# Prompt attention of a hybrid decoder step on one core: group A normalised on its probabilities by GpSimd, group B by spread matmuls as before

## The chip, the cores and the metric

One NeuronCore of a Trainium2 chip runs the whole program. The metric is device time in microseconds of one execution; the time of a kernel is the median of several runs. TensorE (PE) multiplies matrices into PSUM banks, VectorE (DVE) and ScalarE (ACT) read and empty them, GpSimd (POOL) works on SBUF, and SyncE (SP) issues DMAs. Each engine runs its own queue in order, and they wait for one another only through semaphores.

## The reference, cut to what matters

```
m = max(s, axis=-1)                 # group A: also with the head's sink
p = exp(s - m[..., None])
den = sum(p, axis=-1)               # group A: plus exp(sink - m)
o = einsum('nbcgqs,nbscd->nbqcgd', p, vc)
o = o / den                         # one denominator for each query row and head
```

Layer 0 mixes 1,024 prompt tokens with attention of 16 heads of width 64: group A (8 heads, the last 128 keys) and group B (8 heads, three dilated windows, merged into one set of weights). A projection, a pooling layer and two MLPs stand around it, and 64 sample tokens take the same way. All of it is float32.

## The kernel before

The program is a row of stages, each a block of engine queues with a barrier at its end: projection, prompt attention, sample attention, output projection, then a trunk of MLPs and pooling. Only prompt attention (`prompt_attention`) is touched. The next stage issues its loads behind the barrier.

It walks over 8 query tiles of 128 rows, called blocks 0 to 7 here. A block has 16 *steps*, one for each head: steps 0 to 7 are group A (pairs A0 to A3), steps 8 to 15 group B (pairs B0 to B3). A head of group A reads 128 keys in block 0 and 256 in the others; a head of group B reads i + 1 key tiles in block i, up to 1,024 columns.

- PE computes the scores of a pair at each even step (`scores`). Where they are wider than 512 columns (group B of blocks 4 to 7, "wide") they fill all four score banks, and the next `scores` waits until both reductions of the pair before are done (`biased_before`). Narrow scores have two sets of banks and wait for the reductions one pair earlier.
- DVE reduces: one custom instruction adds the bias table, writes the scores to `probs` and the row's extreme to `least` (L886). In group A a copy of one column stands ahead of it (L881). ACT exponentiates the row in place and writes its sum to `den` (L848). `probs` has 7 slots (`SB`); a slot is written again when PE has transposed what it held.
- PE transposes the probabilities, 128 columns at a time (`turn`, L947), about five steps late (`LAG`). ACT or DVE copies the result to `pT` (L832, L899), and PE multiplies it with the values (`multiply`, L966). The work is cut into *groups* of up to two key tiles of a pair. A list gives each group a number n, which decides its PSUM bank (4 + n % 2). PE handles groups in *batches* of two consecutive numbers, 2m and 2m + 1: it transposes both, then multiplies the two groups before them. A batch runs at the step of its second group.
- The denominators belong to query rows, while the outputs lie transposed. So a *spread* group follows the last pair of each 8 heads in that list: 8 matmuls of the reciprocals, broadcast to 64 columns, with the identity (L937). ACT copies the bank to `spread` (L827), and DVE multiplies the outputs of 8 heads by it when it takes them out of PSUM (`take_outputs`, L862).
- POOL computes the low parts of keys and queries (L810): three instructions at step 9 for the next block, one at step 1 for group B.

## Time and profile before

| | |
|---|---|
| median of 3 runs | 2415.77 us (2414.3 to 2416.92) |
| profiled execution, its own time | 2418.88 us |
| its span, first to last instruction | 2416.8 us |
| mean granted TensorE clock | 0.971 of full |
| prompt attention, first scores to last outputs | 271.2 to 467.3 us |

The profile shows one execution. PE's matmuls are pipelined and their ends are modelled, so the distance from one group's start to the next group's start is a better price than a duration. The trace splits the matmuls of a spread group and of `multiply` into two records each: 8 of them are x16 there, while 8 transposes are x8.

### The profile page before, as it was taken

What the parts mean: (1) busy time and instruction counts of PE and PEld (TensorE: products, weight loads), DVE (VectorE), ACT (ScalarE), POOL (GpSimd) and SP (SyncE); (2) the same over time, 40 slices, a digit from 0 to 9 for tenths busy, and PEclk for the clock granted to TensorE, in tenths of its full rate; (3) what the DMA queues carried; (4) which work ended last, traced back from release to release, by engine and by line L of the source; (5) the groups of instructions that cost most, each with busy time, mean ns of one, the idle gap of its engine ahead of it and who ended that gap; (6) DMA issues with size and microseconds to landing.
All of it is one profiled execution on the core that took longest, in us unless ns stands there. A gap on an engine that the chain in (4) does not pass through costs nothing.

```text
span 2416.8 us, 34453 instructions
## 1 busy us (share of the span) xinstructions
PE 2276.5 (94%) x14141; PEld 2047.3 (85%) x14141; DVE 960.3 (40%) x1691; ACT 670.3 (28%) x1305; POOL 156.4 (6%) x200
## 2 busy tenths in 40 slices
PE   6999899878796999999999999989999999999997
PEld 6999777666586998989989988878899898998996
DVE  4200266555453342433433434574334243343345
ACT  4211486433332220311311203253022031131121
POOL 1000121000022000000000000441000000000002
PEclk9999899989898999999999999898999999999999
DMA  4230200298322220210201204122022021020123
GB/s 158 74 92 1 88 2 2 83 331 315 114 87 74 70 62 9 69 46 23 69 21 48 61 9 160 41 97 84 7 70 61 9 69 46 24 69 20 50 86 110
DMA packets 125665, 175.94 MB, mean 73 GB/s; under 512 B 14461, under 2 KB 94389, under 8 KB 125436
## 3 DMA queue, kind: packets, MB, share of 16 engines
q1 hardware_dynamic: 121532, 169.86, 21.5%
q10 hardware_dynamic: 4032, 4.65, 0.6%
q8 instruction: 73, 1.20, 0.2%
q14 instruction: 28, 0.23, 0.0%
HBM read 156.14 MB, written 18.58 MB: 72 GB/s over the span
## 4 chain that ended last, share of the span: by engine, by line
PE 66%; DVE 1%; issue 1%; ACT 0%; POOL 0%; DMA 0%; POOLq 0%; ACTq 0%; DVEq 0%
PE ps L1732 31%; PE ps L1752 31%; PE ps L2238 2%; PE ps L2255 1%; PE ps L1741 1%; DVE t_y L1519 0%; DVE t_zn L1519 0%; PE ps L2266 0%; ACT junk L1507 0%; POOL stats L224 0%; DMA t_raw<-mlp_w 0%; PE ps L1790 0%; DVE m_xT_lo L2149 0%; DVE t_y L1690 0%; DVE t_h_lo L1664 0%
## 5 line engine op out<-in xcount | busy, mean ns | idle before, releaser
L1690 DVE TENSOR_TENSOR t_y<-t_y,ps 128x512 f32<-128x512 f32 x288 | 197.4, 687 | 648.7 <-PE ps L1752 648.5
L1752 PE MATMUL ps<-t_w_hi,t_h_hi 128*128 128x512 f32 x1152 | 451.3, 392 | 3.7 <-DVE t_h_hi L1667 2.2
L1752 PE MATMUL ps<-t_w_lo,t_h_hi 128*128 128x512 f32 x1152 | 449.7, 390 | 0.0
L1752 PE MATMUL ps<-t_w_hi,t_h_lo 128*128 128x512 f32 x1024 | 399.6, 390 | 0.0
L1732 PE MATMUL ps<-m_xT_hi,t_w_hi 128*128 128x384 f32 x1512 | 334.2, 329 | 8.8 <-DVE t_w_lo L1651 8.8
L1732 PE MATMUL ps<-m_xT_lo,t_w_hi 128*128 128x384 f32 x1512 | 333.8, 328 | 0.0
L1732 PE MATMUL ps<-m_xT_hi,t_w_lo 128*128 128x384 f32 x1512 | 333.7, 328 | 0.0
L1621 ACT ACTIVATE t_relu<-ps 128x384 f32<-128x384 f32 (+1 forms) x192 | 87.9, 458 | 820.5 <-PE ps L1752 776.7
L1732 PEld LDWEIGHTS ps<-m_xT_hi,t_w_hi 128*128 128x128 f32 x1512 | 259.6, 188 | 10.3 <-DVE t_w_lo L1651 9.2
L1651 DVE TENSOR_TENSOR t_w_lo<-t_raw,t_w_hi 128x1024 fp32r<-128x1024 f32 x128 | 155.4, 1224 | 284.4 <-ACT t_w_hi L1609 284.0
L1752 PEld LDWEIGHTS ps<-t_w_hi,t_h_hi 128*128 128x128 f32 x1152 | 217.2, 189 | 52.2 <-DVE t_y L1690 3.1
L1732 PEld LDWEIGHTS ps<-m_xT_lo,t_w_hi 128*128 128x128 f32 x1512 | 258.7, 188 | 0.0
L1732 PEld LDWEIGHTS ps<-m_xT_hi,t_w_lo 128*128 128x128 f32 x1512 | 258.7, 188 | 0.0
L1752 PEld LDWEIGHTS ps<-t_w_lo,t_h_hi 128*128 128x128 f32 x1152 | 217.2, 189 | 44.4
L1752 PEld LDWEIGHTS ps<-t_w_hi,t_h_lo 128*128 128x128 f32 x1024 | 193.0, 188 | 40.4
L1609 ACT ACTIVATE t_w_hi<-t_raw 128x1024 fp32r<-128x1024 f32 x128 | 133.7, 1057 | 313.5 <-DMA t_raw<-mlp_w 161.7
L222 POOL TENSOR_SCALAR stats<-stats 128x1 f32<-128x1 f32 x72 | 39.6, 550 | 1731.9 <-ACT junk L1507 1548.5
L1659 DVE TENSOR_TENSOR t_square<-t_relu 128x384 f32<-128x384 f32 (+1 forms) x192 | 101.6, 529 | 39.2 <-ACT t_relu L1621 39.2
L596 PE MATMUL ps<-in_w_hi,a_xT_hi 128*128 128x256 f32 x360 | 105.2, 292 | 1.5 <-DVE a_xT_lo L355 1.5
L596 PE MATMUL ps<-in_w_lo,a_xT_hi 128*128 128x256 f32 x360 | 102.8, 285 | 0.0
L596 PE MATMUL ps<-in_w_hi,a_xT_lo 128*128 128x256 f32 x360 | 102.7, 285 | 0.0
L1664 DVE TENSOR_TENSOR t_h_lo<-t_square,t_h_hi 128x384 fp32r<-128x384 f32 (+1 forms) x192 | 98.7, 514 | 7.3
(201 smaller groups left out, 2624.8 us busy)
## 6 DMA issues: line engine op xcount, KB each, us to landing
t_raw<-mlp_w SPq DMA_DIRECT2D x128, 512.0 KB, 4.1
sa_kb<-cache_b_k SPq DMA_DIRECT2D x40, 512.0 KB, 5.7
sa_vb<-cache_b_v SPq DMA_DIRECT2D x40, 512.0 KB, 8.3
in_raw<-attn_w_in SPq DMA_DIRECT2D x7, 1024.0 KB, 6.8
t_rows<-scratch_x SPq DMA_DIRECT2D x12, 512.0 KB, 5.8
qT<-x_prompt SPq DMA_DIRECT2D x8, 512.0 KB, 3.6
out_rows<-x_prompt SPq DMA_DIRECT2D x8, 512.0 KB, 3.5
scratch_x<-out_rows SPq DMA_DIRECT2D x8, 512.0 KB, 2.6
```

The lines of the kernel that those rows point to most:

```text
L222: nc.gpsimd.tensor_scalar(ms[:, col], ms[:, col], EPS, None, ALU.add).then_inc(shifted, 1)
L596: last = nc.tensor.matmul(core.ps[:, 6 + i % 2, 0:W], a[:, k, c:c + P], b[:, n % 2, k, :], start=(k == 0 and b is w_hi and a is xT_hi), st ...
L1609: self.nc.scalar.activation(self.split_into(n)[0], self.raw_view(n), ACT.Copy).then_inc(self.hi_done, 1)
L1621: nc.scalar.activation(sb.relu[:, n % 2, 0:w], self.core.ps[:, 3 * (i % 2) + j, 0:w], ACT.Relu).then_inc(self.relu_done, 1)
L1651: self.nc.vector.tensor_tensor(lo, self.raw_view(n), hi.bitcast(F32), ALU.subtract).then_inc(self.lo_done, 1)
L1659: nc.vector.tensor_tensor(sb.square[:, n % 2, 0:w], sb.relu[:, n % 2, 0:w], sb.relu[:, n % 2, 0:w], ALU.mult).then_inc(self.squared, 1)
L1664: op = nc.vector.tensor_tensor(sb.h_lo[:, i, c:c + prompt], sb.square[:, n % 2, 0:prompt], sb.h_hi[:, i, c:c + prompt].bitcast(F32), ALU.s ...
L1690: self.nc.vector.tensor_tensor(part, part, self.core.ps[:, 6 + n % 2, :], ALU.add).then_inc(self.part_added, 1)
L1732: mm = self.nc.tensor.matmul(out, a[:, k, :], b_[:, k, c], start=(k == 0 and x == 0), stop=(k == KT - 1 and x == 2))
L1741: mm = self.nc.tensor.matmul(out, a[:, k, :], b_[:, k, c], start=(k == 0 and x == 0), stop=(k == KT - 1 and x == 2))
L1752: mm = self.nc.tensor.matmul(self.core.ps[:, 6 + half, :], a[:, k, t * P:t * P + P], w[:, k, half * 512:(half + 1) * 512], start=(k == 0 a ...
L2238: op = nc.tensor.matmul(pooled_ps(q)[:, f, 0:rhs.shape[-1]], lhs, rhs, start=(j == 0), stop=(j == len(parts) - 1))
```

## The change

The list of groups keeps the spread group behind B3 and drops the one behind A3. For group A, DVE computes the reciprocals of two heads at a time, at the step behind the pair. GpSimd multiplies the pair's two rows of `probs` by them in place (semaphore `normed`), and PE's transposes of a group-A pair wait for that, no longer for the exponentials. DVE takes the outputs of group A with a plain copy.

```diff
--- before.py
+++ after.py
@@ -662,6 +662,8 @@
         biased = core.sem("pa_biased")
         exped = core.sem("pa_exped")
         rden_ready = core.sem("pa_rden_ready")
+        rden_a_ready = core.sem("pa_rden_a_ready")
+        normed = core.sem("pa_normed")
         spread_ready = core.sem("pa_spread_ready")
         turned = core.sem("pa_turned")
         copied = [core.sem("pa_copied_act"), core.sem("pa_copied_dve")]
@@ -690,7 +692,7 @@
         groups = []
         for u in range(0, U, 2):
             groups += [(u, g, min(2, n_tiles(u) - g)) for g in range(0, n_tiles(u), 2)]
-            if u % NH == NH - 2:
+            if u % HEADS == HEADS - 2:
                 groups.append((u, 0, 0))
 
         def is_spread(n):
@@ -755,7 +757,7 @@
         def wait_for_copy(n):
 
             if is_spread(n):
-                nc.tensor.wait_ge(spread_ready, groups[n][0] // NH + 1)
+                nc.tensor.wait_ge(spread_ready, groups[n][0] // HEADS + 1)
             else:
                 mine = [copier[m] for m in range(n + 1) if not is_spread(m)]
                 nc.tensor.wait_ge(copied[copier[n]], mine.count(copier[n]))
@@ -800,7 +802,14 @@
 
             @block.gpsimd
             def _(pool):
-                for step in range(-1, U):
+                for step in range(-1, U + 1):
+                    if 2 <= step <= U and step % 2 == 0 and (step - 2) % HEADS < NH:
+                        i, d = divmod(step - 2, HEADS)
+                        pool.wait_ge(rden_a_ready, i * NH // 2 + d // 2 + 1)
+                        for u in (step - 2, step - 1):
+                            row = probs[:, u % SB, 0:n_tiles(u) * P]
+                            nc.gpsimd.tensor_scalar(row, row, rden[:, i, u % HEADS:u % HEADS + 1], None,
+                                                    ALU.mult).then_inc(normed, 1)
                     for n in split_pieces(step):
                         pool.wait_ge(hi_done, lo_pieces(n + 1))
                         wait_for_scores(pool, n)
@@ -821,9 +830,9 @@
                     u, _, k = groups[n]
                     act.wait_ge(turned, n + 1)
                     if is_spread(n):
-                        x = u // NH
+                        x = u // HEADS
                         if x >= 2:
-                            act.wait_ge(o_taken, x - 1)
+                            act.wait_ge(o_taken, 2 * (x - 1))
                         nc.scalar.activation(spread[:, x % 2, :], core.ps[:, 4 + n % 2, :], ACT.Copy).then_inc(spread_ready, 1)
                         return
                     m = before(n)
@@ -856,9 +865,13 @@
                     i, j, _ = parts_of(u)
                     group = j // 4
                     dve.wait_ge(multiplied, before(turned_after(u)))
-                    x = u // NH
+                    dve.wait_ge(lo_done, lo_pieces(3 * i + 2 + group))
+                    if group == 0:
+                        nc.vector.tensor_copy(qT[:, 0:4, i * P:(i + 1) * P],
+                                              core.ps[:, 6, :].rearrange("p (j c) -> p j c", j=4)).then_inc(o_taken, 1)
+                        return
+                    x = u // HEADS
                     dve.wait_ge(spread_ready, x + 1)
-                    dve.wait_ge(lo_done, lo_pieces(3 * i + 2 + group))
                     nc.vector.tensor_tensor(qT[:, 4 * group:4 * group + 4, i * P:(i + 1) * P],
                                             core.ps[:, 6 + group, :].rearrange("p (j c) -> p j c", j=4),
                                             spread[:, x % 2, :].rearrange("p (j c) -> p j c", j=4), ALU.mult).then_inc(o_taken, 1)
@@ -885,10 +898,14 @@
                             table, start = bias_b[:, h, WB - w:], -NEG
                         nc.vector.tensor_tensor_reduce(probs[:, u % SB, 0:w], score_ps(u), table, -0.125, start,
                                                        ALU.add, ALU.min, least[:, i, d:d + 1]).then_inc(biased, 1)
-                    if 1 <= step <= U and step % NH == 0:
-                        i, d = divmod(step - NH, HEADS)
+                    if 1 <= step <= U and step % HEADS == 0:
+                        i, d = step // HEADS - 1, NH
                         dve.wait_ge(exped, step)
                         nc.vector.reciprocal(rden[:, i, d:d + NH], den[:, i, d:d + NH]).then_inc(rden_ready, 1)
+                    if 2 <= step <= U and step % 2 == 0 and (step - 2) % HEADS < NH:
+                        i, d = divmod(step - 2, HEADS)
+                        dve.wait_ge(exped, step)
+                        nc.vector.reciprocal(rden[:, i, d:d + 2], den[:, i, d:d + 2]).then_inc(rden_a_ready, 1)
                     for n in (n for batch in batches_at(step) for n in batch):
                         if copier[n] == 1:
                             dve.wait_ge(turned, n + 1)
@@ -928,9 +945,9 @@
                     u, g, k = groups[n]
                     if n >= 2:
                         wait_for_copy(n - 2)
+                    i, j, _ = parts_of(u)
                     if is_spread(n):
-                        i, j, _ = parts_of(u)
-                        pe.wait_ge(rden_ready, u // NH + 1)
+                        pe.wait_ge(rden_ready, u // HEADS + 1)
                         for p in range(4):
                             for half in range(2):
                                 d = 2 * (j - 3 + p) + half
@@ -939,7 +956,9 @@
                                                         start=True, stop=True)
                         last.then_inc(turned, 1)
                         return
-                    if g == 0:
+                    if g == 0 and j < 4:
+                        pe.wait_ge(normed, NH * i + 2 * j + 2)
+                    elif g == 0:
                         pe.wait_ge(exped, u + 2)
                     for half in range(2):
                         for t in range(k):
```

Each block has one number fewer in the list. Every block had an even count of groups, so that each began with the first group of a batch; now the groups of blocks 1, 3, 5 and 7 begin with the second. The order of the queues shows it. In the rows below an x8 counts matmuls of the program, and L921, L937, L947 and L966 of before are L938, L954, L966 and L985 of the changed kernel (scores, spread, transposes, multiplications).

PE in block 3 of before, from the scores of A3 (128x256) over those of B0 and B1 (128x512):

```order
L921 MATMUL ps<-pa_k_hi,pa_q_lo 128x256 x2
L947 MATMUL ps<-identity,pa_probs 128x128 x8
L966 MATMUL ps<-pa_pT,v 64x128 x2
L921 MATMUL ps<-pa_k_hi,pa_q_hi 128x512 x2
L921 MATMUL ps<-pa_k_lo,pa_q_hi 128x512 x2
L921 MATMUL ps<-pa_k_hi,pa_q_lo 128x512 x2
```

The same place in the changed kernel:

```order
L938 MATMUL ps<-pa_k_hi,pa_q_lo 128x256 x2
L938 MATMUL ps<-pa_k_hi,pa_q_hi 128x512 x2
L938 MATMUL ps<-pa_k_lo,pa_q_hi 128x512 x2
L938 MATMUL ps<-pa_k_hi,pa_q_lo 128x512 x2
L966 MATMUL ps<-identity,pa_probs 128x128 x8
L985 MATMUL ps<-pa_pT,v 64x128 x4
```

The batch between A3 and B0 (transposes of A0 and A1) is gone from there; the batch behind the scores of B0 now transposes A1 and A2, and A0 went one batch earlier, behind the spread of the block before.

PE in block 7 of before, from the batch behind the scores of A3 to the scores of B2 (wide, 128x512 x4):

```order
L947 MATMUL ps<-identity,pa_probs 128x128 x8
L966 MATMUL ps<-pa_pT,v 64x128 x2
L921 MATMUL ps<-pa_k_hi,pa_q_hi 128x512 x4
L921 MATMUL ps<-pa_k_lo,pa_q_hi 128x512 x4
L921 MATMUL ps<-pa_k_hi,pa_q_lo 128x512 x4
L921 MATMUL ps<-pa_k_hi,pa_q_hi 128x512 x4
L921 MATMUL ps<-pa_k_lo,pa_q_hi 128x512 x4
L921 MATMUL ps<-pa_k_hi,pa_q_lo 128x512 x4
L947 MATMUL ps<-identity,pa_probs 128x128 x8
L966 MATMUL ps<-pa_pT,v 64x128 x8
L921 MATMUL ps<-pa_k_hi,pa_q_hi 128x512 x4
```

The same place in the changed kernel, from the last scores of A3 on:

```order
L938 MATMUL ps<-pa_k_hi,pa_q_lo 128x256 x2
L938 MATMUL ps<-pa_k_hi,pa_q_hi 128x512 x4
L938 MATMUL ps<-pa_k_lo,pa_q_hi 128x512 x4
L938 MATMUL ps<-pa_k_hi,pa_q_lo 128x512 x4
L966 MATMUL ps<-identity,pa_probs 128x128 x8
L985 MATMUL ps<-pa_pT,v 64x128 x4
L938 MATMUL ps<-pa_k_hi,pa_q_hi 128x512 x4
L938 MATMUL ps<-pa_k_lo,pa_q_hi 128x512 x4
L938 MATMUL ps<-pa_k_hi,pa_q_lo 128x512 x4
L938 MATMUL ps<-pa_k_hi,pa_q_hi 128x512 x4
L938 MATMUL ps<-pa_k_lo,pa_q_hi 128x512 x4
L938 MATMUL ps<-pa_k_hi,pa_q_lo 128x512 x4
```

Before, a batch stood ahead of B0's scores, none between B0 and B1, one between B1 and B2. Now none stands ahead of B0's, one between B0 and B1, none between B1 and B2. Block 5 has the same order. In blocks 2, 4 and 6 the batches up to A2 and A3 stand where they stood.

POOL's queue of one block in the changed kernel; before, it held the L810 rows (now L819) alone:

```order
L811 TENSOR_SCALAR pa_probs<-pa_probs,pa_den 128x256 x8
L819 TENSOR_TENSOR pa_k_lo<-kaT,pa_k_hi 128x128
L819 TENSOR_TENSOR pa_k_lo<-kbT,pa_k_hi 128x4x128
L819 TENSOR_TENSOR pa_q_lo<-qT,pa_q_hi 128x512 x2
```

Eight multiplications a block, two each at steps 2, 4, 6 and 8, stand between the low part of step 1 and those of step 9.

## Rows read from the trace of the kernel before

**Rows 1.** Windows: us, busy us by engine (instructions), granted clock, DMA share, GB/s.

```profile
271.00:475.00 204.00, 183.77 (x1972) 145.92 (x1973) 119.58 (x415) 139.19 (x373) 32.03 (x34) 0.94 0.09 31
```

**Rows 2.** Waits in 271 to 468 us: total, times, longest.

```profile
PE ps L921 <- DVE pa_least L886: 10.4, 7, 2.5
PE ps L937 <- ACT pa_pT L832: 3.3, 3, 1.1
PE ps L947 <- ACT pa_probs L848: 0.3, 1, 0.3
```

**Rows 3.** Instruction groups of the stage: busy us, mean ns, idle before.

```profile
L810 POOL TENSOR_TENSOR pa_q_lo<-qT,pa_q_hi 128x512 fp32r<-128x512 f32 x16 | 20.4, 1275 | 61.9 <-ACT pa_q_hi L818 60.1 <-POOL pa_k_lo L810 1.5
L810 POOL TENSOR_TENSOR pa_k_lo<-kaT,pa_k_hi 128x128 fp32r<-128x128 f32 x8 | 3.7, 460 | 278.6 <-ACT pa_k_hi L818 278.6
L891 DVE RECIPROCAL pa_den<-pa_den 128x8 f32<-128x8 f32 x16 | 3.2, 199 | 0.7 <-ACT pa_probs L848 0.6
```

**Rows 4.** Timeline, PE, spread groups of A in blocks 0 and 3.

```profile
280.95 1.97 PE L937 MATMUL ps<-identity,pa_den 128*64 128x128 f32 x16
...
332.38 1.09 PE L937 MATMUL ps<-identity,pa_den 128*64 128x128 f32 x16 [1.13 <-ACT pa_pT L832]
333.40 0.66 PE L947 MATMUL ps<-identity,pa_probs 128*128 128x128 f32 x4
```

**Rows 5.** Timeline, PE, starts of the scores of B0 and B1: block 1, block 3.

```profile
291.81 0.39 PE L921 MATMUL ps<-pa_k_hi,pa_q_hi 64*128 64x256 f32 x2
...
292.27 0.28 PE L921 MATMUL ps<-pa_k_hi,pa_q_hi 64*128 64x256 f32 x2
...
326.64 0.51 PE L921 MATMUL ps<-pa_k_hi,pa_q_hi 64*128 64x512 f32 x2
...
327.44 0.39 PE L921 MATMUL ps<-pa_k_hi,pa_q_hi 64*128 64x512 f32 x2
```

**Rows 6.** Timeline, DVE, two reductions of group A and a reciprocal, block 5.

```profile
362.59 0.15 DVE L881 COPY pa_probs<-pa_neg_sink 128x1 f32<-128x1 f32 x1
...
363.06 0.20 DVE L891 RECIPROCAL pa_den<-pa_den 128x8 f32<-128x8 f32 x1
...
363.60 0.08 DVE L886 DVE_READ_ACCUMULATOR2_ANT pa_least<- 128x1 f32 x1
```

**Rows 7.** One-input POOL instructions: count, ns min/median/max; then busy us, mean ns.

```profile
L222 POOL TENSOR_SCALAR stats<-stats x72: 221/223/1317, 8.4 to 2408.2; 128x1 f32<-128x1 f32 x72
L2012 POOL MEMSET t_y<- 128x9216 f32 x1 | 7.8, 7781 | 9.8 <-DVE t_xn L1519 9.8
```

**Rows 8.** Timeline, two POOL instructions back to back, and the PE start behind the first.

```profile
269.88 2.68 POOL L810 TENSOR_TENSOR pa_q_lo<-qT,pa_q_hi 128x512 fp32r<-128x512 f32 x2
271.19 0.47 PE L921 MATMUL ps<-pa_k_hi,pa_q_hi 64*128 64x128 f32 x2 [6.57 <-POOL pa_q_lo L810]
```

**Rows 9.** Timeline, PE, block 7, from the batch behind A3 to the scores of B3.

```profile
433.89 1.09 PE L947 MATMUL ps<-identity,pa_probs 128*128 128x128 f32 x8
...
435.37 0.72 PE L921 MATMUL ps<-pa_k_hi,pa_q_hi 64*128 64x512 f32 x4
...
439.52 0.74 PE L921 MATMUL ps<-pa_k_hi,pa_q_hi 64*128 64x512 f32 x4 [2.49 <-DVE pa_least L886]
...
443.64 0.74 PE L921 MATMUL ps<-pa_k_hi,pa_q_hi 64*128 64x512 f32 x4 [0.41 <-DVE pa_least L886]
...
445.24 1.09 PE L937 MATMUL ps<-identity,pa_den 128*64 128x128 f32 x16
...
447.88 0.73 PE L921 MATMUL ps<-pa_k_hi,pa_q_hi 64*128 64x512 f32 x4
```

**Rows 10.** Timeline, PE, block 5: scores of B1 and the transposes behind them.

```profile
376.45 0.61 PE L921 MATMUL ps<-pa_k_hi,pa_q_hi 64*128 64x384 f32 x4 [1.98 <-DVE pa_least L886]
...
378.07 1.97 PE L947 MATMUL ps<-identity,pa_probs 128*128 128x128 f32 x8
```

**Rows 11.** Windows: a stretch behind the wait of rows 10.

```profile
378.00:381.00 3.00, 3.00 (x24) 2.60 (x24) 1.93 (x4) 2.53 (x6) 2.50 (x3) 0.57 0.00 0
```

## The prediction, made before the changed kernel ran

> **What bounds the kernel now.** I read the page first, for the span, 2416.8 us, then the windows of prompt attention. That stage takes about a twelfth of the span, and PE is busy for 184 of 204 us in it [rows 1], so most of what PE does there is on the path; the barrier behind it hands any gain or loss on to the end. Next I read PE's waits, because time saved on PE counts only where it doesn't turn into a wait. After start-up there are three kinds [rows 2]: 10.4 us for DVE's reductions, nearly all in the wide part of blocks 4 to 7; 3.3 us for ACT's copies, each just ahead of group A's spread (one wait each in blocks 1, 2 and 3); 0.3 us for exponentials in block 1. Then I went through the timeline block by block and laid the new order of batches over it. E is the moment when PE ends the scores of the pair that I name; a matmul of 128 columns costs 0.128 us, an eighth of a spread group from start to start [rows 4].
>
> **Removed: PE's spreads and their waits.** A spread takes 1.02 us at the full clock (332.38 to 333.40) and, in block 0 at the half clock, 1.9 of its 1.97 us before the next starts [rows 4]; eight together are 7 x 1.02 + 1.9 = 9.0 us. The 3.3 us of waits for ACT end with it: the copies that PE waited for stand behind ACT's splits of step 9, and in the new order PE comes to those banks later or with other work in between. The 0.3 us for the exponentials falls into the new waits below. Together 9.0 + 3.3 + 0.3 = 12.6 us. ACT's eight copies and DVE's changed take are off the path; I give them nothing.
>
> **Added: reciprocals and multiplications.** Eight instead of sixteen long reciprocals stay, and 32 short ones come, 0.2 us each, 0.12 to the next start [rows 3, 6]; they lie in DVE's waits for scores. In the wide part the last one stands where the long one stood. Cost nothing; without that cover 24 x 0.12 = 2.9 us. For a GpSimd multiplication of 128x256 no row exists. From below: a one-input instruction of one column, 0.22 us, plus 256 columns at the 0.84 ns of a memset (7781 / 9216) is 0.44 us [rows 7]. From above: the two-input subtraction takes 0.46 us at 128 and 1.275 at 512 columns, so 0.73 at 256 [rows 3]. I take 0.6, one input but a real operation. The Trainium skill (GPSIMD Engine Reference, section 3.1) gives 1.8 cycles per element as the best of a tight loop and calls VectorE about twice as fast for such work; 256 x 1.8 at 1.2 GHz and the 0.22 of the row would be about 0.6, an estimate, and the sum by it the same.
>
> The multiplication counts only where PE comes too early. DVE begins 0.1 us behind E, reaches the reciprocal 0.47 later and ends it after 0.2 [rows 6]; two multiplications and their gap take 1.3, with handoffs of 0.05 to 0.1 [rows 8]. So the rows are ready at E + 2.15. In the narrow blocks PE is there sooner:
> - Block 1: E of A3, then the scores of B0 (0.46, 291.81 to 292.27) and the transposes of A1 (4 x 0.128 = 0.51): E + 0.97, wait 1.2 [rows 5].
> - Block 2: E of B0; the scores of B1, between 0.46 and 0.8, and the transposes of A2: E + 1.15, wait 1.0.
> - Block 3: E of A3; the scores of B0 take 0.8 [rows 5], then 0.51: E + 1.3, wait 0.85.
> - Block 0, half the columns: two waits of about 0.35, 0.7.
>
> That is 3.8 us, rounded up. In blocks 4 to 7 the wide scores come only after DVE's next reductions, E + 3 or later, and the wait is hidden. If the multiplication were a bare 0.44 or as much as 0.73, the four waits would change by 3.5 x 2 x 0.15 = about 1 us either way.
>
> **Moved: the batches of the odd blocks.** This is the part that gives most back. In block 1 A3 is now multiplied a batch later, behind scores of the next block; DVE, waiting there to take the outputs, begins the next reductions late, and PE waits about 0.6 for them. In blocks 5 and 7 PE's filler moves away from the waits for wide reductions. Before, in block 7, PE had 1.48 us of work ahead of B0's scores, waited 2.49 ahead of B1's, had 2.0 and waited 0.41 ahead of B2's, and 2.64 ahead of B3's (445.24 to 447.88) without a wait [rows 9]. Now nothing stands ahead of B0's: they wait for two reductions and a reciprocal, 0.1 + 1.1 + 0.15 = 1.35 [rows 6]. Ahead of B1's stand 12 matmuls, 1.53, so 0.96 is left of 2.49. Ahead of B2's stands nothing: 2.5. Ahead of B3's stand 16 matmuls, 2.05, against the 2.5 of two bare reductions: 0.45. Waits of 5.3 in place of 2.9: +2.4 us. Block 5 likewise: 1.35 + 0.45 + 2.1, against 1.98 before [rows 10]: +2.0 with a remainder of 0.1. Block 6 loses 0.2 where the spread covered a reduction, block 4 nothing. Without the spread the waits of those blocks also end in work that has already been done, and that is counted: I compared states at the same matmul. Together 0.6 + 2.4 + 2.0 + 0.2 = 5.2 us.
>
> **Sum.** -12.6 + 3.8 + 5.2 = -3.6 us. The profiled execution took 2418.88 us, 3.1 above the median of the runs, and would become 2415.3; against the median of 2415.77 I forecast 2412.2. About 0.2%, 4.8 us, is what a measurement of this kernel can tell from no change.
>
> **Rivals.**
> - *The clock.* Behind the 1.98 us wait of block 5, PE's transposes took 1.97 us in place of 1.09 [rows 10], at a granted clock of 0.57, which is mostly the level of 1.2 GHz [rows 11]; behind the 2.49 of block 7 nothing fell [rows 9]. Such a fall costs about 1.6 us (half of some 3.3). The new waits of 1.35 to 2.5 give it more places, and waits in block 0 may keep the half clock longer. The Trainium skill (TensorE: Matmul & The Clock Gate, HAM oscillation) says that gaps between groups of matmuls can put the clock back each time; by that rule both odd blocks would fall. One or two falls more: 2413.8 to 2415.4. Chance 0.18.
> - *The fall in block 5 goes.* Its wait there is only 0.45 now, and the long one comes elsewhere: -1.6, 2410.6. With it may go part of the narrow waits. Chance 0.14.
> - *The moved batches cost nothing.* If DVE reaches its reductions earlier than I laid out, since the spread no longer holds its slots, the 4.4 us of blocks 5 and 7 and some of block 1 vanish: 2407 to 2408. For it speaks that DVE waits for PE more than PE for DVE; against it that in the wide part the two only alternate. Chance 0.13.
> - *Slower: GpSimd's multiplication.* Each 0.1 us on it lengthens the four narrow waits by 0.2 each, 0.7 in all. It eats the 3.6 us at 0.6 + 0.5 = 1.1 us, and near 2 us for a pair GpSimd would be the bound of the narrow blocks, at PE's own rate there. At 1.3 us each, a whole 128x512 subtraction [rows 3], the time is 2417; beyond that, 2421 and more. No row of such an instruction excludes it. Chance 0.08.
>
> **How the numbers follow.** The forecast's own case, 2410.5 to 2414, has 0.47. Faster by over 0.2% (below 2410.9): the third rival, most of the second and a small part of the forecast, 0.13 + 0.13 + 0.07 = 0.33. Slower (above 2420.6): the worst of the fourth and what I haven't seen, 0.07. The rest, 0.60, is within 0.2%. The range runs from the third rival's 2407.5 to the fourth's 2417, with a tenth left out on either side.
>
> **What the changed profile would show.** PE's record count for spreads halves to 128, and no wait for ACT's copies stands in blocks 1 to 3 at step 13. POOL shows 64 multiplications, 56 of them of 256 columns near 0.6 us; if they are near 1.1, the sum is wrong there. PE waits at the second transposes of the batch for GpSimd in blocks 1, 2 and 3, about 1 us each, and nowhere in blocks 4 to 7. Waits of PE for the reductions rise from 10.4 to about 15 us, in blocks 5 and 7, at the scores of B0 and B2. If these are right and the time still isn't, it is the clock: the mean over the stage, 0.94 now [rows 1], would tell. The forecast fails if the stage's gain is far from 3.6 us, or if later stages differ by more than their own spread between executions.

## The result and the profile after

The changed kernel takes 2422.94 us, the median of 11 runs (2417.7 to 2427.05), beside 2416.92 us for the kernel before, run in turn with it (11 runs, 2414.3 to 2419.12). The ratio is 1.0021, 95% interval 1.0013 to 1.0029: slower by 5.1 us (the two medians lie 6.0 apart), where 3.6 less was forecast. The profiled execution took 2424.55 us, its span is 2422.7.

All of it is in prompt attention: in the two profiled executions, from its first scores to the first instruction of the next stage's queue are 196.9 us before and 203.6 after, and what lies behind is the same within a microsecond. The windows of the stage, of the kernel after, cut where block 4 begins (columns as in [rows 1]):

```profile
271.05:343.27 72.22, 59.43 (x572) 45.56 (x572) 40.30 (x197) 53.31 (x170) 43.67 (x48) 0.86 0.16 60
343.27:474.62 131.35, 117.06 (x1262) 93.89 (x1260) 74.94 (x222) 83.76 (x195) 43.31 (x45) 0.96 0.01 2
271.00:475.00 204.00, 176.48 (x1832) 139.45 (x1832) 115.33 (x418) 137.07 (x364) 87.36 (x96) 0.92 0.06 22
```

The same two pieces of the kernel before:

```profile
271.19:337.51 66.32, 61.23 (x636) 47.57 (x637) 39.73 (x184) 52.98 (x173) 17.12 (x16) 0.90 0.18 65
337.51:468.09 130.58, 120.13 (x1326) 95.91 (x1324) 76.09 (x210) 85.61 (x201) 14.15 (x13) 0.97 0.01 2
```

Blocks 0 to 3 take 5.9 us more, blocks 4 to 7 0.8 more. Within the stage PE is busy for 4.9 us less (176.5 in place of 181.4; the window of [rows 1] takes in some of the next stage) and idle for 11.6 us more. Its waits, of the kernel after, in the stage, beside [rows 2]:

```profile
PE ps L938 <- DVE pa_least L899: 15.1, 13, 2.5
PE ps L966 <- POOL pa_probs L811: 9.6, 8, 1.8
PE ps L954 <- ACT pa_pT L841: 0.4, 1, 0.4
PE ps L966 <- ACT pa_pT L841: 0.3, 1, 0.3
```

The multiplications, of the kernel after, by shape (busy us, mean ns, idle before them):

```profile
L811 POOL TENSOR_SCALAR pa_probs<-pa_probs,pa_den 128x256 f32<-128x256 f32 x56 | 51.1, 927 | 21.6 <-DVE pa_den L908 21.4
L811 POOL TENSOR_SCALAR pa_probs<-pa_probs,pa_den 128x128 f32<-128x128 f32 x8 | 4.7, 609 | 3.3 <-DVE pa_den L908 3.3
```

927 ns, not 600. The timeline of block 1, of the kernel after, shows how it is passed on (start and length in us, engine, line; in brackets the idle time ahead and what ended it):

```profile
288.65 0.17 DVE L908 RECIPROCAL pa_den<-pa_den 128x2 f32<-128x2 f32 x1 [0.20 <-ACT pa_probs L857]
...
289.22 1.27 POOL L819 TENSOR_TENSOR pa_q_lo<-qT,pa_q_hi 128x512 fp32r<-128x512 f32 x1 [5.12 <-ACT pa_q_hi L827]
290.47 3.63 POOL L811 TENSOR_SCALAR pa_probs<-pa_probs,pa_den 128x256 f32<-128x256 f32 x4
...
292.44 0.63 PE L966 MATMUL ps<-identity,pa_probs 128*128 128x128 f32 x4 [1.39 <-POOL pa_probs L811]
...
293.10 0.60 ACT L841 ACTIVATE pa_pT<-ps 128x512 f32<-128x512 f32 x1 [1.41 <-PE ps L966]
...
293.60 0.50 ACT L857 ACTIVATE pa_probs<-pa_probs,pa_least 128x257 f32<-128x257 f32 x1
...
294.24 0.15 DVE L894 COPY pa_probs<-pa_neg_sink 128x1 f32<-128x1 f32 x1 [2.51 <-PE ps L938]
...
294.71 0.16 DVE L908 RECIPROCAL pa_den<-pa_den 128x2 f32<-128x2 f32 x1
...
294.97 3.63 POOL L811 TENSOR_SCALAR pa_probs<-pa_probs,pa_den 128x256 f32<-128x256 f32 x4 [0.87 <-DVE pa_den L908]
...
296.94 0.63 PE L966 MATMUL ps<-identity,pa_probs 128*128 128x128 f32 x4 [1.79 <-POOL pa_probs L811]
```

The reader is to see two things. The first pair's reciprocal ran at 288.65, but its multiplication begins only at 290.47: the low parts of q stand ahead of it in POOL's queue, and they waited for ACT until 289.22 and then took 1.27 us. And one late multiplication makes the next one late. PE, held up until 292.44, computes its next scores late. DVE waits 2.51 us for these (294.24), and the next reciprocal, which stands behind their reduction in DVE's queue, runs at 294.71. ACT's exponentials are late as well (293.60), behind a copy that waited 1.41 us for PE's transposes, but they end half a microsecond before that reciprocal. The next multiplication begins at 294.97, and PE waits 1.79 us again.

### The profile page after: what moved, and what is told of

The parts are those of the page before. It is cut to its first block, busy times and chain, and to the rows that moved or that the text cites. A ratio compares the mean times of both kernels' runs of the same rounds, so it can differ in the third digit from the quotient of the medians.

```text
span 2422.7 us, 34261 instructions
## 1 busy us (share of the span) xinstructions
PE 2268.1 (94%) x14013; PEld 2040.1 (84%) x14013; DVE 960.2 (40%) x1715; ACT 668.8 (28%) x1297; POOL 211.3 (9%) x264
## 3 DMA queue, kind: packets, MB, share of 16 engines
q8 instruction: 72, 1.18, 0.2%
## 4 chain that ended last, share of the span: by engine, by line
PE 65%; DVE 1%; issue 1%; ACT 0%; POOL 0%; DMA 0%; POOLq 0%; ACTq 0%; DVEq 0%
PE ps L1751 31%; PE ps L1771 31%; PE ps L2257 2%; PE ps L2274 1%; PE ps L1760 0%; DVE t_y L1538 0%; PE ps L2285 0%; DMA t_raw<-mlp_w 0%; DVE t_zn L1538 0%; ACT junk L1526 0%; POOL stats L224 0%; PE ps L1809 0%; DVE m_xT_lo L2168 0%; DVE t_y L1709 0%; DVE t_h_lo L1683 0%
## 5 line engine op out<-in xcount | busy, mean ns | idle before, releaser
L1751 PEld LDWEIGHTS ps<-m_xT_hi,t_w_hi 128*128 128x128 f32 x1512 | 259.8, 188 | 11.6 <-DVE t_w_lo L1670 10.6
```

The costliest lines, as they stand in the source:

```text
L1751: mm = self.nc.tensor.matmul(out, a[:, k, :], b_[:, k, c], start=(k == 0 and x == 0), stop=(k == KT - 1 and x == 2))
```

## The experiments

Each ratio is to the kernel before, run in turn on the same chip; "against before" is that ratio less one, times 2417 us. An interval is about 2.4 us either side (4 for those of 4 runs, 3 for the 6 of e11, 2 for the kernel after), so a difference of two rows is known to about 3 us. The last two columns are lengths in the one profiled execution: first scores to the first scores of block 4, and from there to the stage's end. For the same code in blocks 0 to 3 they differ by 1.4 us (before, e9) and 1.7 us (e12, e3). What lies behind the stage, the same code in every kernel, took from 1942.7 to 1950.2 us in these executions.

| kernel | median us (runs) | ratio (95%) | against before, us | blocks 0-3 | blocks 4-7 |
|---|---|---|---|---|---|
| before | 2416.92 (11) | 1 | 0 | 66.3 | 130.6 |
| after | 2422.94 (11) | 1.0021 (1.0013-1.0029) | +5.1 | 72.2 | 131.4 |
| e1_dve_mult | 2426.63 (4) | 1.0044 (1.0027-1.0061) | +10.6 | 70.7 | 136.7 |
| e2_no_mult | 2415.3 (10) | 0.9995 (0.9986-1.0005) | -1.2 | 65.5 | 130.8 |
| e3_even | 2419.73 (10) | 1.0015 (1.0006-1.0025) | +3.6 | 74.7 | 128.4 |
| e4_even_no_mult | 2414.68 (10) | 0.9993 (0.9983-1.0002) | -1.7 | 67.8 | 128.3 |
| e5_after_warm | 2421.86 (10) | 1.0021 (1.0011-1.003) | +5.1 | 72.6 | 131.2 |
| e6_before_warm | 2416.94 (10) | 1.0002 (0.9992-1.0011) | +0.5 | 63.5 | 131.9 |
| e7_per_head | 2419.18 (10) | 1.0009 (0.9999-1.0019) | +2.2 | 69.5 | 131.2 |
| e8_double | 2459.19 (4) | 1.0169 (1.0152-1.0186) | +40.8 | 96.9 | 143.0 |
| e9_wide_blocks | 2414.79 (10) | 0.9995 (0.9986-1.0005) | -1.2 | 67.7 | 127.3 |
| e12_narrow_blocks | 2427.08 (4) | 1.0046 (1.003-1.0063) | +11.1 | 73.0 | 130.4 |
| e10_no_mult_warm | 2413.9 (10) | 0.9988 (0.9979-0.9998) | -2.9 | 64.6 | 129.5 |
| e11_spreads_twice | 2425.35 (6) | 1.0036 (1.0023-1.0049) | +8.7 | 70.0 | 133.6 |
| e13_lag7_before | 2421.69 (10) | 1.0016 (1.0006-1.0026) | +3.9 | 65.5 | 137.5 |
| e14_lag7_no_mult | 2417.89 (10) | 0.9997 (0.9988-1.0007) | -0.7 | 64.1 | 134.4 |
| e15_lag7_after | 2418.16 (10) | 1.0004 (0.9994-1.0013) | +1.0 | 62.3 | 139.5 |
| e16_lag7_even | 2417.48 (10) | 0.9995 (0.9985-1.0004) | -1.2 | 64.4 | 134.0 |
| e17_lag_even | 2416.74 (11) | 1.0 (0.9991-1.0009) | 0 | 63.8 | 132.6 |
| e18_lag_before | 2420.37 (11) | 1.0012 (1.0003-1.0021) | +2.9 | 64.9 | 134.7 |

### The change taken apart: e1 to e4

**e1_dve_mult.** The multiplication moves from GpSimd to VectorE, behind its reciprocal.

```diff
-                            nc.gpsimd.tensor_scalar(row, row, rden[...], None, ALU.mult).then_inc(normed, 1)
+                            nc.vector.tensor_scalar(row, row, rden[...], None, ALU.mult).then_inc(normed, 1)
```

> The multiplications of group A's probabilities move from GpSimd to VectorE, right behind the reciprocals; everything else as in the changed kernel. Theory 1 (GpSimd's multiplication, 0.93 us where I had taken 0.6, holds PE back: 10.8 us of waits for it in the changed profile): VectorE does one in 0.2 to 0.4 us, PE's waits for the multiplication nearly vanish and the time falls to 2410 to 2414. Theory 2 (the batches moved by the new list cost it, whoever multiplies): 2418 to 2423, with the waits for reductions as they are. Theory 3 (VectorE's own queue is too full for 56 more instructions): PE's waits for the reductions grow by about what those for the multiplication shrink, 2418 or more.

Worse than the change, by 5.5 us. The instruction is short there, 369 ns on the mean, but VectorE's queue is the one that PE waits for; of e1, the group and PE's waits:

```profile
L905 DVE TENSOR_SCALAR pa_probs<-pa_probs,pa_den 128x256 f32<-128x256 f32 (+1 forms) x64 | 20.9, 369 | 1.1
...
PE ps L936 <- DVE pa_least L892: 21.6, 18, 2.9
PE ps L964 <- DVE pa_probs L905: 1.2, 3, 0.5
```

Waits for the multiplication are nearly gone (1.2 us), those for the reductions are 6.5 us more than in the kernel after, and blocks 4 to 7 lose 5. So taking the multiplication away from GpSimd and giving it to VectorE is no remedy.

**e2_no_mult.** The changed kernel without any multiplication; group A's outputs stay undivided.

```diff
-                            nc.gpsimd.tensor_scalar(row, row, rden[...], None, ALU.mult).then_inc(normed, 1)
-                    if g == 0 and j < 4:
-                        pe.wait_ge(normed, NH * i + 2 * j + 2)
-                    elif g == 0:
+                    if g == 0:
```

> The changed kernel without the multiplications: group A is left without its normalisation, PE's transposes of group A wait for the exponentials as before, the reciprocals and the new order of batches stay. Theory 1: all that GpSimd cost is gone, 10.8 us of waits and one or two clock falls, so 2409 to 2412, and about my forecast's other terms (12.6 saved, 5.2 given back: 2416.9 - 7.4 = 2409.5). Theory 2 (the moved batches): 2416 or more.

**e3_even.** The change, with a blank number where the spread stood, so that batches and PSUM banks are those of before.

```diff
             if u % HEADS == HEADS - 2:
                 groups.append((u, 0, 0))
+            elif u % NH == NH - 2:
+                groups.append((u, 0, -1))
```

> The changed kernel with an empty number in the list of groups where group A's spread stood, so that every block keeps an even count and the batches and banks stand as before the change; GpSimd multiplies as in the changed kernel. Theory 1: the order gives back about 5 us of the forecast's terms, but PE waits for GpSimd in each narrow block as before: 2417 to 2420. Theory 2 (order is what costs): 2411 or less.

**e4_even_no_mult.** Both edits: the kernel before less its eight spreads, again with group A's outputs undivided. The 32 short reciprocals of the changed kernel stay in e2 and e4.

> As the one before, but without the multiplications (group A is left without its normalisation) and with PE waiting for the exponentials as before: the kernel before, less eight spreads. Both theories expect the whole of what a spread costs on PE: 8 x 1.02 to 9.0 us, and up to 3.3 us of waits for ACT's copies: 2404.5 to 2408. Against the run with the new order and no multiplications it shows what the order alone costs: 5 us by my forecast, 0 to 1 if the moved batches cost nothing.

The three part the sum, each difference to about 3 us. The spreads' removal gives 1.7 us (interval -0.5 to 4.1), not 12.6. The reciprocals are inside this figure: 24 more instructions on VectorE, which the prediction put at nothing and without cover at 2.9 us, and no run left them out. The new batches cost 0.5 (e2 against e4) or 1.5 (after against e3), not 5.2. The multiplication costs 5.3 (e3 against e4) or 6.3 (after against e2), not 3.8. PE's waits of e4:

```profile
PE ps L945 <- DVE pa_least L906: 12.0, 10, 2.5
PE ps L973 <- ACT pa_pT L848: 4.7, 3, 1.6
```

The waits for ACT's copies that stood ahead of the spreads, 3.3 us in [rows 2], have not gone with them: one stands ahead of the next transposes in each of blocks 1, 2 and 3, and they are 4.7 us.

### The clock: e5, e6, e10

Over all runs so far the span times one minus the mean granted clock was 3.3 us higher after than before, and 3.5 in e4 (3.2 in e3, so the multiplication did not add to it there). I took it for the price of the clock, and tested it by holding the clock up at the stage's start.

```diff
+                filler(30)
                 for step in range(STEPS):
                     if step < U and step % 2 == 0:
                         scores(step)
+                        if step == 2:
+                            filler(8)
```

`filler(n)` is n transposes of the identity into a PSUM bank that isn't in use. **e5_after_warm** has it in the changed kernel, **e6_before_warm** in the kernel before.

> The changed kernel with 38 transposes of the identity more on PE, whose results nothing reads: 30 at the start of the stage, where PE waits for the first low parts (6.6 us), and 8 behind the scores of step 2, ahead of a wait. Theory (part of the loss is the clock: over all executions so far the span times one minus the mean granted clock is 71.7 us for the changed kernel and 68.4 for the one before): the low stretch at the stage's start, 20.5 us, shrinks by 10 us or more, block 0's matmuls take half the time, and the time falls by 4 to 8 us, to 2415 to 2419. Rival (block 0 goes at the pace of DVE and ACT, and the clock only changes where PE waits): PE's waits in block 0 grow by what its matmuls save, and the time stays at 2421 to 2424, or rises by the filler's own 4 us.

> The kernel before with the same 38 filler transposes. Theory: its low stretch at the stage's start, 17.1 us, shrinks as well, and the time falls to 2408 to 2412. As both kernels now start the stage at the full clock, the changed one with filler should stand only the part that isn't clock behind this one: 2.5 to 3.5 us in place of 5.7. Rival: no gain, 2415 to 2418, and the distance between the two stays near 5.7.

**e10_no_mult_warm** has it in e4.

> The kernel before without group A's spreads and without any multiplication by the reciprocal for those heads (2414.7 as measured), with the 38 filler transposes at the start of the stage. In the profile of the version without filler, block 1 took 18.8 us in place of 14.9, at a granted clock of 0.71. Theory (the clock takes back the credit of the spreads): the low stretch goes, block 1 takes 14 to 15 us and the time falls by 4 to 6 us, to 2409 to 2411. Rival (other executions have no such stretch, or PE waits for ACT and DVE instead, as with the filler in the kernel before, which gained nothing): 2413 to 2416.

In e6 the granted clock of the first 14 us is 0.98 in place of 0.50; the window of e6, then the same of before:

```profile
271.00:285.00 14.00, 11.71 (x124) 8.81 (x122) 7.04 (x50) 9.63 (x41) 4.47 (x5) 0.98 0.81 302
```

```profile
271.00:285.00 14.00, 12.54 (x88) 10.02 (x90) 5.31 (x39) 8.73 (x36) 4.41 (x5) 0.50 0.81 301
```

PE gets through 124 matmuls, 8 of them filler, instead of 88, block 0 takes 11.1 us instead of 13.9, and yet the median is that of before; in the profile blocks 4 to 7 give half of it back. In e5 the level of 1.2 GHz only came later, from 276 us, and nothing was gained; in e10 1.2 us were, inside the interval, and in its profile block 1 still had a clock of 0.82. The falls of 4 us and more that the theory expected of e5 and e6 are excluded. A smaller share of the clock is not: the filler held the level up in e6 alone, and there it cost PE 1.1 us of its own behind step 2.

The profiles say more. Take the length of the stage apart into the time in which PE is idle, what the level of 1.2 GHz adds (at most the length times one minus the granted clock, summed over the blocks), and the rest, which is PE's work at the full clock:

| kernel | stage, us | PE idle | added by the low level | rest |
|---|---|---|---|---|
| before | 196.9 | 15.5 | 10.3 | 171.0 |
| after | 203.6 | 27.1 | 15.4 | 161.1 |
| e2_no_mult | 196.3 | 22.0 | 12.5 | 161.8 |
| e3_even | 203.1 | 23.2 | 17.3 | 162.6 |
| e4_even_no_mult | 196.2 | 18.3 | 15.7 | 162.2 |
| e11_spreads_twice | 203.5 | 15.5 | 10.2 | 177.9 |
| e13_lag7_before | 203.0 | 18.6 | 14.1 | 170.3 |
| e14_lag7_no_mult | 198.5 | 20.9 | 15.6 | 162.0 |

The windows of e4, cut where block 4 begins:

```profile
271.40:339.24 67.84, 61.52 (x572) 47.58 (x572) 40.90 (x196) 51.41 (x169) 17.13 (x16) 0.82 0.17 64
339.24:467.56 128.32, 116.34 (x1262) 92.41 (x1260) 76.75 (x222) 83.69 (x197) 14.20 (x13) 0.97 0.01 1
```

Those of e13 and e14, which are described below, cut in the same way:

```profile
271.39:336.91 65.52, 59.58 (x620) 46.43 (x620) 39.59 (x183) 53.22 (x173) 17.19 (x16) 0.89 0.18 66
336.91:474.40 137.49, 124.86 (x1342) 99.57 (x1340) 76.36 (x210) 85.01 (x200) 14.20 (x13) 0.95 0.01 2
```

```profile
271.57:335.63 64.06, 57.47 (x557) 44.51 (x558) 40.59 (x195) 51.84 (x170) 17.14 (x16) 0.85 0.18 67
335.63:470.04 134.41, 120.13 (x1278) 95.57 (x1276) 76.75 (x222) 82.61 (x194) 14.19 (x13) 0.96 0.01 1
```

In e4 PE's work did fall by 8.8 us, the eight spreads. Of these 2.8 came back as idle time and 5.4 as time at the low level, which in sum is what blocks 0 and 1 have more. In the changed kernel the work fell by 9.9, the idle time rose by 11.6 and the low level's share by 5.1. Each row is one execution, and that of e4 was 3.7 us above its median. Over the 123 runs of the kernel before that were taken beside the experiments, a microsecond more of this measure goes with 0.58 us more time (correlation 0.80), which would put the 3.5 us of e4 at some 2 us: an estimate, and a correlation is no proof of the cause. So the clock stays open as one of the takers of the spreads' credit. What the shorter falls behind the waits of later blocks cost was not isolated.

### The multiplication's size and place: e7, e8, e9, e12

**e7_per_head** takes reciprocal and multiplication one head at a time, a step after its exponentials.

```diff
-                    if 2 <= step <= U and step % 2 == 0 and (step - 2) % HEADS < NH:
+                    if 1 <= step <= U and (step - 1) % HEADS < NH:
...
-                        nc.vector.reciprocal(rden[:, i, d:d + 2], den[:, i, d:d + 2]).then_inc(rden_a_ready, 1)
+                        nc.vector.reciprocal(rden[:, i, d:d + 1], den[:, i, d:d + 1]).then_inc(rden_a_ready, 1)
```

> The changed kernel with reciprocal and GpSimd multiplication one head at a time, each a step after its exponentials, so that the first head of a pair is multiplied while the second one's exponentials still run. DVE has 64 short reciprocals in place of 32. The second head's row is ready about 0.9 us (one multiplication) sooner. Theory (the loss of blocks 0 to 3 is the time from exponentials to multiplied rows): PE's waits for POOL in the stage, 9.6 us in 8, fall to 2 to 5, and the time by 3 to 6 us, to 2417 to 2420. Rival (the waits only move to ACT and DVE, as the waits for ACT's copies did, or 32 more instructions on DVE delay its reductions): 2421 to 2424 with as much waiting in all.

2.9 us better than the change, though the intervals touch. PE's waits for POOL, of e7:

```profile
PE ps L965 <- POOL pa_probs L811: 3.9, 6, 1.2
PE ps L965 <- ACT pa_pT L840: 1.2, 1, 1.2
```

5.7 us of them are gone and half of that shows in the time: the theory had the direction, and the rival its share. The other half stands as waits that the kernel after doesn't have, 1.8 us for POOL's low parts of q at the start of block 2 and 1.2 us for a copy of ACT's in block 3.

**e8_double** multiplies each row again, by 1.0.

```diff
-                                                    ALU.mult).then_inc(normed, 1)
+                                                    ALU.mult).then_inc(once, 1)
+                            pool.wait_ge(once, NH * i + u % HEADS + 1)
+                            nc.gpsimd.tensor_scalar(row, row, 1.0, None, ALU.mult).then_inc(normed, 1)
```

> The changed kernel with a second GpSimd multiplication of each row, by 1.0, behind the first: each pair's rows are ready about 1.9 us later (two more of 0.93), and POOL has 64 instructions and some 56 us more in the stage. Theory (the multiplication's length is passed on to PE in the narrow blocks alone): 8 to 12 waits grow by 1.9 us each and the wide blocks hide it, plus 15 to 23 us and what the clock then loses, 2438 to 2450. Rival (the mechanism isn't the length: queue and handoff set the waits): less than plus 8, below 2431. If the low parts of the next block, which stand behind it on POOL, come late as well: above 2450, and in the wide blocks too.

```profile
L815 POOL TENSOR_SCALAR pa_probs<-pa_probs 128x256 f32<-128x256 f32 x56 | 47.5, 848 | 4.6
...
PE ps L969 <- POOL pa_probs L815: 34.2, 18, 3.4
```

51.7 us more on POOL (these and eight short ones) cost 35.7 us, more than the theory's 15 to 23. PE's waits for it go from 8 to 18, and the longest from 1.8 to 3.4 us; 12 of them, 25.7 us, are in blocks 0 to 3. The other 6, 8.5 us, are in blocks 4 to 7, which hid the single multiplication and don't hide this one: they take 11.6 us more than in the kernel after. Its waits for the low parts of q are as before. The prediction had 0.7 us for each 0.1 on an instruction; the slope here is 35.7 / 8.1, 4.4 for each 0.1, since nearly every pair of the narrow blocks waits and, as the timeline of block 1 showed, each wait delays the next.

**e9_wide_blocks** and **e12_narrow_blocks** are e3 with the change in four blocks only; the others keep their spreads.

```diff
-            if u % HEADS == HEADS - 2:
-                groups.append((u, 0, 0))
-            elif u % NH == NH - 2:
-                groups.append((u, 0, -1))
+            if u % NH == NH - 2:
+                groups.append((u, 0, 0 if u % HEADS == HEADS - 2 or old(u) else -1))
```

> The change in blocks 4 to 7 alone, with the batches and PSUM banks of the kernel before; blocks 0 to 3 keep group A's spreads. Theory (the loss comes from GpSimd's multiplications in the narrow blocks, and a spread less in a wide block is worth part of its 1.0 us): no wait of PE for the multiplications in the stage, no loss, the time 0 to 3 us below the kernel before, 2414 to 2417. Rival (the wide blocks lose as well, for the gaps that the spreads leave lower the clock there): 2418 to 2420.

> The counterpart: the change in blocks 0 to 3 alone, again with the batches and banks of before; blocks 4 to 7 keep their spreads. Theory: PE's 9 us of waits for the multiplications are all here, and with them the loss: 2420 to 2423, as much as the even-batch version of the change (2419.7) or a little more. Rival (the loss is spread over all blocks): 2417 to 2419.

The wide blocks lose nothing measurable: e9 has no wait for POOL, and stands at -1.2. The loss is in the narrow ones, with 9.2 us of such waits in e12. The median of e12 is no measure of its size: the four runs lie between 2419.04 and 2428.8, and +11.1 doesn't fit the +3.6 of e3, which has the same narrow blocks. In its profiled execution, the fastest of the four, the stage takes 203.4 us, 6.5 more than before, and that of e3 takes 203.1.

### What takes the spreads' credit: e11, and a longer distance

**e11_spreads_twice** issues the eight spreads twice.

```diff
-                        for p in range(4):
+                        for p in [*range(4)] * (2 if j < 4 else 1):
```

> The kernel before with group A's eight spreads issued twice each, 64 matmuls and 9.0 us of PE work more (the second writes the same numbers again). Taking them away was worth 2 us. Theory (PE bounds the stage now, and ACT and DVE, at 83 and 65 per cent in the narrow blocks, stand close behind, so that PE work has its price when added and not when removed): plus 6 to 9 us, 2423 to 2426. Rival (the spreads lie in slack that PE has anyway, at most places): plus 0 to 3 us, 2417 to 2420.

9.0 us of PE work added cost 8.7; the same work taken away gave 1.7. I took the kernels with filler to have left the clock out as the reason, which they had not. I gave the transposes a distance of 7 heads behind the scores in place of 5, so that the chain from scores to transposes has more time. Theory (a) is that the length of this chain holds the credit back, (b) that it is the throughput of ACT and DVE.

```diff
-    SB = 7
-    LAG = 5
+    SB = 9
+    LAG = 7
```

> The kernel before with transposes and multiplications 7 heads behind the scores in place of 5, and 9 row buffers in place of 7; nothing else. Control: PE is busy for 90 per cent of the stage and has only 0.3 us of waits for exponentials. By (a), the length of the chain, there is little to gain here: 2414 to 2418. By (b), throughput: the same, 2415 to 2419. A rise beyond 2419 would be the price of filling and draining two more heads, to be taken off the other three.

> The same distance of 7 in the kernel before without group A's spreads and without any multiplication for those heads (2414.7 at a distance of 5). By (a): the waits for ACT's copies, 4.7 us, and what else PE lost behind the exponentials go, and the spreads' 9 us come back at least by half: 2408 to 2411, counted from the control. By (b): the waits stay in the stage under whatever name, 2413 to 2416.

> The changed kernel at a distance of 7 (2422.9 at 5, with 9.6 us of waits of PE for the multiplications). By (a): those waits go to below 1.5 us, and the time falls to 2412 to 2417. By (b): the waits for the multiplications go as well, since two heads are more than their length, but come back as waits for ACT and DVE: 2419 to 2423.

> The change with the batches and PSUM banks of the kernel before (2419.7 at a distance of 5), at a distance of 7. By (a): the multiplication costs nothing any more, and this one stands within 2 us of the one without multiplication, 2409 to 2413, below both kernels. By (b): 2416 to 2420.

At this distance the multiplication costs nothing measurable (e16 against e14: -0.5), where it cost 5.3. Of (a) the waits for the multiplication came out, the times didn't: e14, e15 and e16 stand 6.9, 1.2 and 4.5 us above its figures (the kernel before stood at 2418.18 us on that chip), and e14 still waits 4.4 us for ACT's copies. Theory (b) had the time of e16 alone. PE's waits of e15, the changed kernel at 7:

```profile
PE ps L938 <- DVE pa_least L899: 16.7, 12, 2.5
PE ps L966 <- ACT pa_pT L841: 3.4, 4, 1.1
```

No wait for POOL is left of 9.6 us, 3.4 us of ACT's came in their place, and blocks 0 to 3 take 62.3 us instead of 72.2. In e16, with the batches of before, four waits for POOL of 2.5 us in all remain, in blocks 1 and 2. Without any multiplication the spreads' removal is worth 4.6 us (e14 against e13) in place of 1.7, a difference that the intervals don't tell from none; by the table above PE gets 2.3 us more idle time in return for them, about as much as at 5 heads (2.8), and 1.5 us at the low level in place of 5.4. But the distance itself costs 3.9 us (e13). In its profile that is block 7, which takes 53.7 us in place of 47.8; no other block differs by more than 1.4.

**e17_lag_even** and **e18_lag_before** keep 7 up to block 6 and take 5 in the last, to spare the longer drain.

```diff
+        def lag(u):
+            return LAG if u < U - HEADS else LAG - 2
```

> The change with the batches and banks of before, at a distance of 7 heads in blocks 0 to 6 and of 5 in the last. Theory (the price of the distance is the drain of the last block): 5 to 6 us below the version with 7 throughout (2417.5), so 2411 to 2413, 4 to 6 below the kernel before. Rival (the distance costs elsewhere as well): 2415 to 2417.

> The kernel before with the same two distances: what the distance alone gives. Theory: the 4.3 us of the version with 7 throughout go, 2415 to 2417, so that what e17 stands below it, 3.5 to 5 us, is the worth of the change itself once the multiplication is off the path (forecast: 12.6 without its waits and its moved batches). Rival (the distance alone is the gain): as fast as e17, and the change is worth nothing.

The change is worth 2.9 us here (e17 against e18), with intervals that touch. The distance's cost went from 3.9 to 2.9 in the medians, less than the intervals can tell, and in the profiles block 7 went from 53.7 to 51.0 us, still above the 47.8 of before: part of the cost was the drain, how much is open. e17 came out where the rival had it, e18 above both figures, and no version beat the kernel before by more than 0.2%. A distance of 7 in blocks 0 to 3 and 5 from there on wasn't tried.

## Why the prediction was wrong

- **Removed, 12.6 us.** This is the step that failed: "Together 9.0 + 3.3 + 0.3 = 12.6 us." Measured 1.7 (e4, with the short reciprocals in it), 10.9 less. It took "most of what PE does there is on the path" as valid in both directions. e11 shows that it holds for work added. For work removed the profile of e4 shows where the time went. The 3.3 us of waits for ACT's copies belonged to the copies, not to the spreads: they moved to the next transposes and became 4.7. The waits for reductions rose from 10.4 to 12.0. And PE spent more time at the low level, 5.4 us by that one execution, about 2 by the estimate from all runs. What caused the last is open; so are the share of the short reciprocals, and that of ACT, which is busy for 53 of 66 us in blocks 0 to 3 of before. That a chain too short for 5 heads held back some 3 us, as e13 and e14 had seemed to say, is not shown.
- **Added, 3.8 us.** Measured 5.3 to 6.3. The blocks were right, none in 4 to 7, the count was not: five waits were laid out, two in block 0 and one in each of 1 to 3, and there are eight, of 9.6 us in all (0.47 and 0.58 in block 0, 1.39 and 1.79 in block 1, 1.17, 1.18 and 1.62 in block 2, 1.45 in block 3). Nor was the size of the instruction, 0.93 for 0.6: its upper bound, 0.73 by the two-input subtraction, was no bound, since that takes 2.1 ns for each further column [rows 3] and the multiplication 2.5. By the prediction's own 0.7 for each 0.1 the 0.93 give 2.3 more, and 6.1; that this meets the measured time is partly luck, as it is the sum of five waits. Two things were left out and show in the timeline: POOL's low parts ahead of the first multiplication of block 1, and the way in which a late multiplication, by way of PE's scores and DVE's queue, makes the next one late. The Trainium skill (GPSIMD Engine Reference, section 3.1) gives 1.8 cycles per element at best, at 1.2 GHz, from which 1.5 ns is an estimate; here 128 more columns take 318 ns (927 less 609), 2.5 ns each, so the trace doesn't agree with it for this form.
- **Moved, 5.2 us.** Measured 0.5 to 1.5. In the profile the holes stand where they were laid out: at the scores of block 5 waits of 1.26, 0.35 and 1.93 (forecast 1.35, 0.45, 2.1), in block 7 of 1.26, 0.91, 2.47 and 0.42 (1.35, 0.96, 2.5, 0.45), and the waits for reductions are 15.1 us (about 15). These of the kernel after, in block 7:

```profile
441.53 0.73 PE L938 MATMUL ps<-pa_k_hi,pa_q_hi 64*128 64x512 f32 x4 [1.26 <-DVE pa_least L899]
...
449.81 0.73 PE L938 MATMUL ps<-pa_k_hi,pa_q_hi 64*128 64x512 f32 x4 [2.47 <-DVE pa_least L899]
```

  As a count of waits it was the best part of the prediction; as a difference in time it was too high. Without the spreads the old batches have more of these waits as well (12.0 us in e4, 12.1 in e3), so the new ones add 3 us, not 5. In the table of the stage the new batches add 3.7 and 3.9 us of idle time (e2 beside e4, after beside e3), and the low level adds 3.2 and 1.9 us less in those executions.
- **Rivals.** The clock, at +1.6 for each fall, was what I turned to first. The filler excluded it as the whole of the loss and left a share open. The falls were expected in both odd wide blocks: block 5 has its own as before (transposes of 1.97 us at 388.05), block 7 has none, and what is more than before lies in blocks 1 and 4, whose clocks are 0.83 and 0.93 in place of 1.00. The slower case was rightly named as GpSimd's multiplication, but with the point from which it decides at 1.1 us: at 0.93 it cost more than the removal gave, because the removal gave 1.7.
- **Sum.** -1.7 + 0.5 + 6.3 = +5.1 by e4, e2 and the result, for -12.6 + 5.2 + 3.8 = -3.6: 10.9 and 2.5 too hopeful, 4.7 too dark. Each difference is known to about 3 us; only the first error is well beyond that, the third a little.

## What to carry to other kernels

An engine that is busy for 90% of a stage can pay in full for work that is added and give back little of what is taken away, here 1.7 us of 9.0. Before crediting a removal, ask which wait will stand at the next instruction instead: a wait for another engine's copy doesn't go with the instruction that happens to wait for it. An operation put into the chain between two engines is priced by its latency, the queue ahead of it included, against the distance of the pipeline. It cost nothing measurable where the distance had room (blocks 4 to 7, or 7 heads), and was multiplied where each late item delays the next. A higher share at the low clock in a slower run is no proof that the clock made it slower; and a filler that doesn't hold the clock up in the kernel in question is no proof that it didn't.

## What the runs showed of the hardware

- GpSimd multiplies 128x256 fp32 by a scalar per partition in 927 ns and 128x128 in 609; by the constant 1.0 in 848 and 529 (e8). The scalar from a tile costs 75 to 80 ns. On VectorE the same two take 381 and 284 ns (e1).
- VectorE's instructions did not get slower beside 56 us more of GpSimd's in the stage: the copy of one column ahead of a reduction has a mean of 148 ns after, and the reduction of 128x256 478 ns, as before within 2 ns.
- At the stage's start PE works at the 1.2 GHz level, and how soon it leaves it differs between kernels. These windows are of e5, where 30 transposes ran ahead of the first scores: the clock was full at first, PE busy for 2.46 of 4.5 us, and then fell for the next 13 us.

```profile
271.00:275.50 4.50, 2.46 (x26) 2.01 (x26) 1.30 (x11) 0.96 (x5) 1.61 (x2) 1.00 0.72 243
276.00:289.00 13.00, 11.84 (x73) 8.77 (x74) 6.34 (x42) 8.74 (x37) 7.46 (x11) 0.50 0.59 230
```

  With the same filler and no waits for GpSimd e6 had 0.98 over the first 14 us. In e4, without filler, the level lasted from 271 to beyond 291 us:

```profile
271.00:291.00 20.00, 18.00 (x122) 14.19 (x124) 9.75 (x67) 12.53 (x51) 5.88 (x6) 0.50 0.57 213
```
